# A fourth pair of steps in three feed-forward stages, and two of a pair's weight sums made ahead in DRAM

## The chip, the cores and the metric

One core of a Trainium2 chip runs the whole program. The metric is the device time of one execution in microseconds. Every time of the profile is counted from the start of the span of one profiled execution.

## The reference

Two blocks of a transformer in float32 over 256 positions of width 1024: a gated delta rule, two memory attentions, latent attention, a hybrid mixer, and five feed-forward parts. The change touches the feed-forward parts alone, and where their weights come from:

```python
def swiglu(x, w_gu, w_down):
    gate, up = jnp.split(x @ w_gu, 2, axis=-1)
    return (jax.nn.silu(gate) * up) @ w_down

x = x + 0.5 * swiglu(rms_norm(x, ffn1_norm[l]), ffn1_w_gu[l], ffn1_w_down[l])   # D_MODEL 1024, D_FF 2816
```

## The kernel before

The program is a list of phases (`PHASES`, line 71): ffn0, ain (the delta rule's projections; the recurrence itself runs between them), mem (keys and values of the memories), out0, ffn1, ffn2, bin, uq, out1, ffn3, in2, out2, ffn4. Each phase reads weight tiles of 128 x 2048 float32, 1 MB each. The order of all work is written out by hand, for each engine its own list, and semaphores join the lists.

**A weight tile's way.** SP loads it into one of three raw buffers (`w_raw`, a ring, line 542) when the tile three places before it in the ring has been split (`w_split`). ScalarE rounds it to its high part (`w_hi`, line 584), VectorE takes the rest as its low part (`w_lo`, line 1492). Both parts have three buffers too, so the high part of unit n waits until TensorE has left unit n - 3 (`tile_used`). TensorE does each product as three matmuls: high by high, high by low, low by high (lines 2451 to 2453), with 512 columns in the feed-forward stages.

**A feed-forward stage** has 11 steps of 256 hidden columns. A plain step is two gate-and-up units `g0`, `g1` (for the two halves of the inner dimension, 24 matmuls each) and a down unit `d` (24). Between them four transposes turn the hidden block (lines 2542 and 2602). ffn0, ffn1, ffn3 and ffn4 are `PAIRED`: steps 3 and 4, 6 and 7, 9 and 10 are done as pairs. For a pair, rows (two blocks of 128 positions), inner dimension (two halves) and columns (two steps) form a 2 x 2 by 2 x 2 block product, done with seven products of 12 matmuls in place of eight (Winograd's form): m1, m2, m4 on plain inputs, m6, m7, p3, p5 on sums of inputs (`s_hi_part`, `s_lo_part`), and m4, m6, m7, p5 also on sums of weights. The sums of results (`c11`, `c22`, `c12`) are made by VectorE from snapshots of PSUM that ScalarE takes (`snap`).

**The sums of weights** come in three ways. T1 and T3 are differences of two stored tiles, made in SBUF by GpSimd's queue: a plain load and then a DMA that adds (`pair_sums`, lines 3628 to 3640). T2 = T1 + block and T4 = T2 + block are made by VectorE (`t2`, line 1584, `t4`, line 1590). SP loads the three single blocks into their own buffers (`pair_load`, line 511), so of a pair's weights only the down tiles go through the ring.

**Queues.** SP's loads are one queue, first in, first out. GpSimd's DMAs are another; both share the same 16 DMA engines. ScalarE's and VectorE's lists are in order too: what stands behind a waiting `w_hi` waits with it. In the tail of a stage, ScalarE's order is the last down tile's high part, the next phase's first tile (`w_hi(ends[name])`), then `hidden_hi(10)`. In ain and mem, ScalarE's `w_hi(n0 + 14)` to `w_hi(n0 + 18)` (the four memory tiles and the first of out0) stand between the copies `level_p1` of the delta rule's chain (line 961).

Of the kernel before, what the change touches and what calls it, by code (L numbers as in the profile page):

```python
# [12 lines left out]
P = 128  # L13
SEQ = 256
TB = SEQ // P
# [57 lines left out]
PAIRED = ("ffn0", "ffn1", "ffn3", "ffn4")  # L73
# [25 lines left out]

def stored_at(kind, s):  # L100

    if kind == "d":
        return 3 * STEPS - 1 if s == STEPS - 1 else 3 * s + 4
    return (0 if s == 0 else 3 * s - 1) + int(kind[1])
# [87 lines left out]
def program(nc, d, out):  # L192
# [6 lines left out]
    for name, n in PHASES:  # L199
        tile0[name], stored0[name] = n_tiles, n_stored  # L200
        if name.startswith("ffn"):
            for kind, s in paired_order() if name in PAIRED else plain_order():
                unit_of[name, kind, s] = n_tiles
                if kind in ("g0", "g1", "d"):
                    ring.append((n_tiles, n_stored + stored_at(kind, s)))
# [17 lines left out]
    def last_use(name, half):  # L223

        b = before[name]
        if b.startswith("ffn"):
            return unit_of[b, "p3", STEPS - 2] + 1 if b in PAIRED else unit_of[b, f"g{half}", STEPS - 1] + 1
# [6 lines left out]
    bias_rows = nc.dram_tensor("bias_rows", [P * (ROW + 1)], f32, kind="Internal")  # L234

    with ExitStack() as ctx:
# [81 lines left out]
        PB = [area(S_AT + 2 * TILE + k * TILE, TILE) for k in range(4)]  # L318
        SQ = area(AR_N - 2 * D, TB, D)
# [132 lines left out]

        def pair_no(name, s):
            return len(PAIR_STEPS) * PAIRED.index(name) + PAIR_STEPS.index(s)

        def gates_to(f, s, tb):
            return TB * STEPS * f + GATE_ORDER.index((s, tb)) + 1

        def hiddens_to(f, s, tb):
            return TB * STEPS * f + HIDDEN_ORDER.index((s, tb)) + 1  # L460
# [5 lines left out]
        def pair_source(name, kind, s):  # L466

            if kind == "p5":
# [32 lines left out]
        def _(sp):  # L501
# [11 lines left out]
            def first_loads(kind, name):  # L513

                if kind == "g1":
                    if name != "ffn0":
                        sp.wait_ge(S["x_ready"], 4 * (X_OF[name] - 1) + 1)
                    if name == "ffn3":
                        sp.wait_ge(S["bias_dma"], 16)
                    pair_load(name, PAIR_STEPS[0], 0)  # L520
                    pair_load(name, PAIR_STEPS[0], 2)
                else:
                    sp.wait_ge(S["norm_sd"], norm_no[name] + 1)
                    pair_load(name, PAIR_STEPS[0], 3)

# [11 lines left out]
            for r in range(1, len(ring)):  # L537
                n, t = ring[r]
                if r >= RING:
                    sp.wait_ge(S["w_split"], ring[r - RING][0] + 1)  # L540
                w = width(n)
                sp.dma_start(RAW[:, r % RING, 0:w], d["tiles"][t, :, 0:w]).then_inc(w_loaded[r % RING], 16)
                for name in PAIRED:
# [19 lines left out]
        def _(act):  # L563
# [22 lines left out]
            def pair_ready(name, kind, s):  # L586

                if kind in ("p5", "m7"):
# [91 lines left out]
            def paired_ffn(f, name, first, side):  # L680
# [143 lines left out]
                hidden_hi(10)  # L824
                w_hi(ends[name] + 1)
# [332 lines left out]
            paired_ffn(1, "ffn1", lambda: norm("ffn1"), lambda part: None)  # L1158
# [178 lines left out]
            paired_ffn(3, "ffn3", lambda: norm("ffn3"), lambda part: None)  # L1337
# [130 lines left out]
            paired_ffn(4, "ffn4", lambda: norm("ffn4"), lambda part: None)  # L1468
# [8 lines left out]
        def _(dve):  # L1477
# [81 lines left out]
            def paired_ffn(f, name, start, first, side):  # L1559
# [154 lines left out]
                hidden_lo(10)  # L1714

# [2049 lines left out]
```

## Time and profile before

| | |
|---|---|
| median of 3 runs | 1301.13 us (1301.01 to 1303.16) |
| the profiled execution | 1300.3 us |
| its span | 1298.3 us |
| TensorE busy | 1281.1 us, 99% |
| VectorE busy | 934.5 us, 72% |
| ScalarE busy | 801.0 us, 62% |
| DMA, mean over the span | 205 GB/s, 265.83 MB |
| granted TensorE clock | full, in all slices |

The busy line says which engine's work fills the span; the chain says what the end was waiting for. Since records of matmuls overlap, the distance between two starts is what a matmul costs, and a group's mean is longer. The stages lie at 0 to 192 us (ffn0), 193 to 379 (ain, mem, out0), 379 to 559 (ffn1), 559 to 740 (ffn2), 823 to 1003 (ffn3), 1003 to 1119 (in2, out2) and 1119 to the end (ffn4).

### The profile page before, as it was taken

The page shows a single profiled execution, that of the slowest core. Times are in us where ns is not written, and L with a number is a line of the kernel's source. Part 1 is how long each engine was busy: PE and PEld are TensorE (multiplying, and loading weights), DVE is VectorE, ACT ScalarE, POOL GpSimd, SP SyncE. Part 2 cuts the span into 40 slices and gives each one's busy share as a digit, 9 for nine tenths or more (in the row PEclk, how much of TensorE's full clock was granted, in tenths as well). Part 3 has the DMA queues.
Part 4 walks back from the last instruction along what each step waited for, and adds up shares of the span by engine and source line. Part 5 has one row for each costly group of instructions (what it writes and reads, how often), then busy time and mean ns, then how long its engine had stood idle before and what let it go on. Part 6 is the DMA issues. An engine that isn't in the chain of part 4 may idle for free.

```text
span 1298.3 us, 17145 instructions
## 1 busy us (share of the span) xinstructions
PE 1281.1 (99%) x6976; PEld 1071.9 (83%) x6976; DVE 934.5 (72%) x1091; ACT 801.0 (62%) x1046; POOL 39.8 (3%) x61
## 2 busy tenths in 40 slices
PE   7999999999999999999999999999999999999998
PEld 6888888888988888888787888888888898788887
DVE  5887777777567877866353557678878798688785
ACT  7576658766556665684443466576556757755653
POOL 0000000000000000000000000001000000000000
PEclk9999999999999999999999999999999999999999
DMA  9987635432159778455444532498893534689761
GB/s 354 294 322 227 231 125 195 163 111 87 48 209 339 233 262 290 171 214 202 147 167 146 194 127 73 169 356 260 256 319 103 206 132 151 265 232 328 231 219 33
DMA packets 40206, 265.83 MB, mean 205 GB/s; under 512 B 4476, under 2 KB 6780, under 8 KB 9152
## 3 DMA queue, kind: packets, MB, share of 16 engines
q1 hardware_dynamic: 31056, 205.71, 42.4%
q0 software_dynamic: 7920, 56.37, 16.3%
q10 hardware_dynamic: 1152, 2.66, 0.6%
q8 instruction: 55, 0.90, 0.3%
q14 instruction: 23, 0.19, 0.0%
HBM read 263.67 MB, written 2.11 MB: 205 GB/s over the span
## 4 chain that ended last, share of the span: by engine, by line
PE 95%; ACT 2%; DVE 2%; issue 1%; DMA 0%; SPq 0%; ACTq 0%; DVEq 0%
PE ps L2451 25%; PE ps L2452 25%; PE ps L2453 25%; PE ps L2366 8%; PE ps L2602 1%; PE ps L2377 1%; PE ps L2492 1%; PE ps L2484 1%; PE ps L2497 1%; PE ps L485 1%; PE ps L2507 1%; PE ps L487 1%; PE ps L486 1%; ACT w_hi_part L584 1%; PE ps L2424 1%
## 5 line engine op out<-in xcount | busy, mean ns | idle before, releaser
L1492 DVE TENSOR_TENSOR w_lo_part<-w_raw,w_hi_part 128x2048 fp32r<-128x2048 f32 (+2 forms) x160 | 361.3, 2262 | 135.3 <-ACT w_hi_part L584 135.3
L584 ACT ACTIVATE w_hi_part<-w_raw 128x2048 fp32r<-128x2048 f32 (+2 forms) x159 | 301.4, 1896 | 156.2 <-PE ps L2453 135.1
L2451 PE MATMUL ps<-w_hi_part,x_hi 128*128 128x512 f32 (+1 forms) x800 | 312.3, 390 | 0.8 <-DVE w_lo_part L1492 0.5
L2453 PE MATMUL ps<-w_hi_part,x_lo 128*128 128x512 f32 (+1 forms) x800 | 305.5, 382 | 0.0
L2452 PE MATMUL ps<-w_lo_part,x_hi 128*128 128x512 f32 (+1 forms) x800 | 304.8, 381 | 0.0
L584 ACT ACTIVATE w_hi_part<-arena 128x2048 fp32r<-128x2048 f32 x72 | 138.1, 1918 | 97.4 <-PE ps L2453 93.1
L1492 DVE TENSOR_TENSOR w_lo_part<-arena,w_hi_part 128x2048 fp32r<-128x2048 f32 x72 | 164.6, 2288 | 39.4 <-ACT w_hi_part L584 39.4
L2451 PE MATMUL ps<-w_hi_part,h_hi_part 128*128 128x512 f32 x464 | 186.7, 402 | 0.1
L2453 PE MATMUL ps<-w_hi_part,h_lo_part 128*128 128x512 f32 x464 | 181.4, 391 | 0.0
L2452 PE MATMUL ps<-w_lo_part,h_hi_part 128*128 128x512 f32 x464 | 181.0, 390 | 0.0
L2453 PEld LDWEIGHTS ps<-w_hi_part,x_lo 128*128 128x128 f32 x800 | 150.4, 188 | 29.8
L2451 PEld LDWEIGHTS ps<-w_hi_part,x_hi 128*128 128x128 f32 x800 | 150.5, 188 | 29.5 <-ACT arena L714 1.5
L2452 PEld LDWEIGHTS ps<-w_lo_part,x_hi 128*128 128x128 f32 x800 | 150.7, 188 | 26.7
L2451 PEld LDWEIGHTS ps<-w_hi_part,h_hi_part 128*128 128x128 f32 x464 | 87.2, 188 | 19.3 <-issue 1.9
L2453 PEld LDWEIGHTS ps<-w_hi_part,h_lo_part 128*128 128x128 f32 x464 | 87.1, 188 | 19.0
L2452 PEld LDWEIGHTS ps<-w_lo_part,h_hi_part 128*128 128x128 f32 x464 | 87.2, 188 | 17.7 <-issue 0.5
L2452 PE MATMUL ps<-w_lo_part,s_hi_part 128*128 128x512 f32 x192 | 76.5, 399 | 0.0
L2451 PE MATMUL ps<-w_hi_part,s_hi_part 128*128 128x512 f32 x192 | 75.8, 395 | 0.0
L2453 PE MATMUL ps<-w_hi_part,s_lo_part 128*128 128x512 f32 x192 | 75.3, 392 | 0.0
L2366 PE MATMUL ps<-arena 64*64 64x64 f32 (+7 forms) x636 | 67.6, 278 | 1.6 <-DVE arena L1829 0.8
L2366 PEld LDWEIGHTS ps<-arena 128*128 128x128 f32 (+3 forms) x636 | 54.9, 164 | 9.6 <-issue 3.9
L2451 PEld LDWEIGHTS ps<-w_hi_part,s_hi_part 128*128 128x128 f32 x192 | 36.1, 188 | 9.0
(443 smaller groups left out, 1555.9 us busy)
## 6 DMA issues: line engine op xcount, KB each, us to landing
w_raw<-in_tiles SPq DMA_DIRECT2D x155, 1024.0 KB, 4.9
arena<-in_tiles SPq DMA_DIRECT2D x36, 1024.0 KB, 6.4
arena<-in_tiles POOLq DMA_DIRECT2D x24, 1024.0 KB, 9.6
t<-in_tiles POOLq DMA_DIRECT2D x18, 1024.0 KB, 10.3
mem_kv<-in_tiles POOLq DMA_DIRECT2D x6, 1024.0 KB, 10.4
w_raw<-in_tiles SPq DMA_DIRECT2D x3, 512.0 KB, 5.9
arena<-in_w_ukv POOLq DMA_DIRECT2D x1, 1536.0 KB, 14.3
arena<-in_w_dkv POOLq DMA_DIRECT2D x1, 1280.0 KB, 8.7
```

The source lines that it names most:

```text
L485: nc.tensor.matmul(o, w_hi, a_hi, start=start, stop=False, skip_group_check=True)
L486: nc.tensor.matmul(o, w_hi, a_lo, start=False, stop=False, skip_group_check=True)
L487: return nc.tensor.matmul(o, w_lo, a_hi, start=False, stop=stop, skip_group_check=True)
L584: nc.scalar.activation(WH[:, n % RING, 0:w], source(n), ACT.Copy).then_inc(S["w_hi"], 1)
L1492: nc.vector.tensor_tensor(WL[:, n % RING, 0:w], source(n), WH[:, n % RING, 0:w], ALU.subtract).then_inc(S["w_split"], 1)
L2366: return nc.tensor.matmul(o, w, a, start=start, stop=stop, skip_group_check=True)
L2377: last = nc.tensor.transpose(bank(2 * tb + half)[:, k * P:(k + 1) * P], X[:, tb, kb * P:(kb + 1) * P], con("ident"))
L2424: nc.tensor.matmul(outs[f], part[:, n % RING, at:at + P], XH[:, 4 * g + k, :], start=g == 0 and k == 0 and part is WH, stop=False, skip_gr ...
L2451: nc.tensor.matmul(o, a_hi, w_hi, start=start, stop=False, skip_group_check=True)
L2452: nc.tensor.matmul(o, a_hi, w_lo, start=False, stop=False, skip_group_check=True)
L2453: return nc.tensor.matmul(o, a_lo, w_hi, start=False, stop=stop, skip_group_check=True)
L2484: nc.tensor.matmul(bank(gu_bank(0, tb)), XH[:, 4 * g + k, tb * P:(tb + 1) * P], WH[:, n % RING, k * 512:(k + 1) * 512], start=g == 0 and k ...
```

## The change

ffn1, ffn3 and ffn4 are taken out of `PAIRED` and become `QUADS`: steps 3 and 4, 5 and 6, 7 and 8, 9 and 10 are done as four pairs, one behind the other, with plain steps only for 0, 1 and 2. ffn0 keeps three pairs. In a quad, a pair's products stand in another order (p5, m2, m1, p3, m6, m7, m4, with the down steps of the pair before between them), m2, m1 and p3 read single stored tiles that now go through the ring, and the down step of 9 is the last of the stage.

T1 and T3 of the quads are made in DRAM, in a tensor of their own (`made_sums`, 24 blocks of 1 MB). SP copies the 24 first blocks there: 8 for ffn1 in ffn0's tail, 16 for ffn3 and ffn4 behind the four memory tiles. GpSimd's queue then adds the other blocks in DRAM, 8 for each stage, paced by the splits of ain, ffn2 and in2. In a quad, SP loads the finished sums (`t_load`). T2 is made by VectorE from T1 and the raw tile of p3, in place, and T4 by a DMA of GpSimd's queue that adds a stored tile to it.

```diff
-PAIRED = ("ffn0", "ffn1", "ffn3", "ffn4")
+PAIRED = ("ffn0",)
+QUADS = ("ffn1", "ffn3", "ffn4")
+QUAD_STEPS = (3, 5, 7, 9)
...
+def quad_order():
+    order = [("g0", 0), ("g1", 0), ("g0", 1), ("g1", 1), ("d", 0), ("g0", 2), ("g1", 2)]
+    for s in QUAD_STEPS:
+        order += [("p5", s), ("m2", s), ("m1", s), ("p3", s), ("m6", s), ("d", s - 2), ("m7", s), ("d", s - 1), ("m4", s)]
+    return order + [("d", 10), ("d", 9)]
...
+def ring_kinds(name):
+    return ("g0", "g1", "d", "m1", "m2", "p3") if name in QUADS else ("g0", "g1", "d")
...
+    made = nc.dram_tensor("made_sums", [len(QUADS) * len(QUAD_STEPS), 2, P, TILE], f32, kind="Internal")
...
 SP
+            def copies_after(n):
+                if n == unit_of["ffn0", "d", 8]:
+                    return range(0, 2)
+                if n == unit_of["ffn0", "d", 9]:
+                    return range(2, 5)
+                if n == unit_of["ffn0", "d", 10]:
+                    return range(5, 8)
+                if tile0["mem"] <= n < ends["mem"]:
+                    return range(8 + 4 * (n - tile0["mem"]), 12 + 4 * (n - tile0["mem"]))
+                return ()
+            def copy_block(i):
...
+                sp.dma_start(made[q, k, :, :], d["tiles"][t, :, :], max_dma_last_dim=4 * TILE).then_inc(q_loaded[3], 16)
+            def t_load(name, s, k):
+                dst, (sem, _) = ((TA[QUAD_STEPS.index(s) % 2], t1_loaded(name, s)), (TC, t3_loaded(name, s)))[k]
+                sp.dma_start(dst, made[quad_no(name, s), k, :, :]).then_inc(sem, 16)
...
+                for c in copies_after(n):
+                    if c == 0:
+                        sp.wait_ge(S["w_split"], unit_of["ffn0", "m2", PAIR_STEPS[-1]] + 1)
+                    copy_block(c)
+                for name in QUADS:
+                    if n == unit_of[name, "g1", 1]:
+                        sp.wait_ge(*made_all(name))
+                        sp.wait_ge(S["x_ready"], 4 * (X_OF[name] - 1) + 1)
+                        t_load(name, QUAD_STEPS[0], 0)
...
+                    for s in QUAD_STEPS[1:]:
+                        if n == unit_of[name, "p3", s]:
+                            sp.wait_ge(S["w_split"], unit_of[name, "m7", s - 2] + 1)
+                            t_load(name, s, 1)
...
 VectorE
+                def t2(s):
+                    r = ring_no[at("p3", s)]
+                    dve.wait_ge(S["w_split"], at("p5", s) + 1)
+                    dve.wait_ge(w_loaded[r % RING], 16 * (r // RING + 1))
+                    a = pair_source(name, "m6", s)
+                    nc.vector.tensor_tensor(a, a, RAW[:, r % RING, :], ALU.add).then_inc(S["sums"], 1)
...
 TensorE
+                def quad_of_steps(s):
+                    if s == QUAD_STEPS[0]:
+                        pe.wait_ge(S["sums"], sum_no[name, "s_lo", 0])
+                    s_product("p5", s, 7, True, False)
+                    turn_pair(s - 1 if s == QUAD_STEPS[0] else s - 2)
+                    x_product("m2", s, 5, 0, 1, True, True)
+                    if s > QUAD_STEPS[0]:
+                        turn_pair(s - 1)
+                    x_product("m1", s, 4, 0, 0, True, False)
+                    pe.wait_ge(S["snap"], snaps_to(name, s, 1))
+                    s_product("p3", s, 7, False, True)
+                    pe.wait_ge(S["sums"], sum_no[name, "c11", s])
+                    s_product("m6", s, 4, False, False)
+                    down_half(s - 2, 0)
+                    down_half(s - 2, 1)
+                    pe.wait_ge(S["sums"], sum_no[name, "c12", s])
+                    s_product("m7", s, 4, False, False)
+                    down_half(s - 1, 0)
+                    down_half(s - 1, 1)
+                    if s == QUAD_STEPS[-1]:
+                        turn_pair(10)
+                    pe.wait_ge(S["sums"], sum_no[name, "c22", s])
+                    x_product("m4", s, 4, 1, 1, False, True)
...
 GpSimd
+            def make_sums(name, copied, paced):
+                pool.wait_ge(S["q_loaded3"], 16 * (n_pairs + 2 * len(QUAD_STEPS) * copied))
+                for i, n in enumerate(paced):
+                    s, k = QUAD_STEPS[i // 2], i % 2
+                    pool.wait_ge(S["w_split"], n + 1)
+                    pool.dma_start(made[quad_no(name, s), k, :, :], stored(name, ("g0", "g1")[k], s + 1), accum_op=ALU.add,
+                                   max_dma_last_dim=4 * TILE).then_inc(S["base_loaded"], 16)
+            def t4_sums(name):
+                for s in QUAD_STEPS:
+                    split(name, "m6", s)
+                    pool.dma_start(TA[QUAD_STEPS.index(s) % 2], stored(name, "g1", s), accum_op=ALU.add).then_inc(t4_added(name, s)[0], 16)
...
-            for s in PAIR_STEPS:
-                pair_sums("ffn1", s)
+            make_sums("ffn1", 1, range(tile0["ain"] + 1, tile0["ain"] + 9))
+            t4_sums("ffn1")
...
+            make_sums("ffn3", 3, range(tile0["ffn2"] + 2, tile0["ffn2"] + 26, 3))
...
-            pair_sums("ffn3", PAIR_STEPS[0])
-            pool.wait_ge(S["tile_used"], tile0["ffn3"] + 8)
+            t4_sums("ffn3")
             pool.dma_start(bass.AP(bias_rows, 0, [[ROW + 1, P], [1, ROW]]),
...
+            make_sums("ffn4", 3, range(tile0["in2"] + 1, tile0["in2"] + 9))
+            t4_sums("ffn4")
```

SP's queue, from the last single loads of ffn0 on, before. The block of 24 loads is the rest of ain, mem, out0 and the first units of ffn1; `arena` is the pairs' buffers.

```order
L542 DMA w_raw<-in_tiles 128x2048
L511 DMA arena<-in_tiles 128x2048 x2
L542 DMA w_raw<-in_tiles 128x2048 x4
L542 DMA w_raw<-in_tiles 128x1072 x2
L542 DMA w_raw<-in_tiles 128x2048 x24
```

The same place now. The two loads of 1072 columns are ain's first tiles.

```order
L629 DMA w_raw<-in_tiles 128x2048 x2
L603 DMA made_sums<-in_tiles 128x2048 x2
L629 DMA w_raw<-in_tiles 128x2048
L603 DMA made_sums<-in_tiles 128x2048 x3
L629 DMA w_raw<-in_tiles 128x2048
L603 DMA made_sums<-in_tiles 128x2048 x3
L629 DMA w_raw<-in_tiles 128x1072 x2
L629 DMA w_raw<-in_tiles 128x2048 x13
```

Eight copies now stand between ffn0's last down tiles and ain's first tile. SP's queue in the part behind, whose 13 loads end with the first memory tile (before, all of it is in the row of 24):

```order
L603 DMA made_sums<-in_tiles 128x2048 x4
L629 DMA w_raw<-in_tiles 128x2048
L603 DMA made_sums<-in_tiles 128x2048 x4
L629 DMA w_raw<-in_tiles 128x2048
L603 DMA made_sums<-in_tiles 128x2048 x4
L629 DMA w_raw<-in_tiles 128x2048
L603 DMA made_sums<-in_tiles 128x2048 x4
L629 DMA w_raw<-in_tiles 128x2048 x8
L608 DMA arena<-made_sums 128x2048
```

Four copies stand behind each memory tile, and out0's first tile is the first of the row of eight. VectorE in ffn1's second pair before; L1590 is the sum t4, L1595, L1600 and L1604 are the corrections, L1618 the low part of a hidden block, L1609 a hidden product:

```order
L1492 TENSOR_TENSOR w_lo_part<-w_raw,w_hi_part 128x2048
L1590 TENSOR_TENSOR arena<-arena 128x2048
L1492 TENSOR_TENSOR w_lo_part<-arena,w_hi_part 128x2048
L1595 TENSOR_TENSOR arena<-arena,ps 128x512
L1492 TENSOR_TENSOR w_lo_part<-t,w_hi_part 128x2048
L1618 TENSOR_TENSOR h_lo_part<-ps,h_hi_part 128x512
L1492 TENSOR_TENSOR w_lo_part<-w_raw,w_hi_part 128x2048
L1492 TENSOR_TENSOR w_lo_part<-arena,w_hi_part 128x2048 x2
L1600 TENSOR_TENSOR arena<-ps,arena 128x512
```

VectorE around the second to third pair of ffn1 now, from the correction c22 to m6's low part (L2000 is t2, L2020 a hidden product, L2015 c22, L2029 a hidden block's low part):

```order
L2015 TENSOR_TENSOR arena<-arena,ps 128x512
L1753 TENSOR_TENSOR w_lo_part<-arena,w_hi_part 128x2048 x2
L2000 TENSOR_TENSOR arena<-arena,w_raw 128x2048
L1753 TENSOR_TENSOR w_lo_part<-w_raw,w_hi_part 128x2048
L2020 SCALAR_TENSOR_TENSOR arena<-ps,norm_rsv,arena 128x256
L2020 SCALAR_TENSOR_TENSOR arena<-arena,norm_rsv 128x256
L1753 TENSOR_TENSOR w_lo_part<-w_raw,w_hi_part 128x2048
L2029 TENSOR_TENSOR h_lo_part<-ps,h_hi_part 128x512
L1753 TENSOR_TENSOR w_lo_part<-w_raw,w_hi_part 128x2048
L1753 TENSOR_TENSOR w_lo_part<-arena,w_hi_part 128x2048
```

One sum per pair (t2) is left to VectorE in place of two; it stands between the low parts of p5 and m2, and the two hidden products that the next transposes need stand behind m2's.

## Rows read from the trace of the kernel before

**Rows 1.** The page: busy time per engine, and the chain's shares by engine.

```profile
PE 1281.1 (99%) x6976; PEld 1071.9 (83%) x6976; DVE 934.5 (72%) x1091; ACT 801.0 (62%) x1046; POOL 39.8 (3%) x61
...
PE 95%; ACT 2%; DVE 2%; issue 1%; DMA 0%; SPq 0%; ACTq 0%; DVEq 0%
```

**Rows 2.** Busy time by window: window, length, engines, clock, DMA share, GB/s.

```profile
378.90:558.70 179.80, 179.80 (x820) 147.64 (x817) 142.70 (x122) 111.83 (x115) 9.61 (x14) 1.00 0.78 267
...
555.00:740.00 185.00, 185.00 (x831) 150.56 (x830) 94.83 (x104) 92.21 (x122) 1.07 (x2) 1.00 0.50 175
194.00:355.00 161.00, 156.40 (x1538) 139.35 (x1536) 115.03 (x222) 109.75 (x182) 0.00 (x0) 1.00 0.33 119
```

**Rows 3.** TensorE's timeline in ffn1: start, length, engine, line, shape, count.

```profile
384.94 1.98 PE L2484 MATMUL ps<-w_hi_part,x_hi 128*128 128x512 f32 x8
386.75 1.98 PE L2492 MATMUL ps<-w_lo_part,x_hi 128*128 128x512 f32 x8
```

**Rows 4.** Groups by shape, VectorE, 380 to 540 us: busy us, mean ns.

```profile
L1492 DVE TENSOR_TENSOR w_lo_part<-arena,w_hi_part 128x2048 fp32r<-128x2048 f32 x18 | 41.2, 2288 | 9.7 <-ACT w_hi_part L584 9.7
...
L1584 DVE TENSOR_TENSOR arena<-t,arena 128x2048 f32<-128x2048 f32 x3 | 6.9, 2284 | 0.1
...
L1618 DVE TENSOR_TENSOR h_lo_part<-ps,h_hi_part 128x512 fp32r<-128x512 f32 x9 | 6.2, 685 | 3.8 <-ACT h_hi_part L727 3.8
```

**Rows 5.** VectorE's timeline in ffn1.

```profile
416.68 2.28 DVE L1492 TENSOR_TENSOR w_lo_part<-arena,w_hi_part 128x2048 fp32r<-128x2048 f32 x1
418.88 0.48 DVE L1609 SCALAR_TENSOR_TENSOR arena<-ps,norm_rsv,arena 128x256 f32<-128x256 f32 x1
```

**Rows 6.** Groups by shape, ScalarE, 380 to 540 us.

```profile
L584 ACT ACTIVATE w_hi_part<-arena 128x2048 fp32r<-128x2048 f32 x18 | 34.5, 1918 | 25.9 <-PE ps L2453 25.4 <-DMA arena<-in_tiles 0.5
...
L714 ACT ACTIVATE arena<-ps 128x512 f32<-128x512 f32 x9 | 5.3, 586 | 1.8 <-PE ps L2453 1.8
```

**Rows 7.** Line 3640, the DMAs that add into SBUF, 12 of them.

```profile
DMA to landing us min/median/max: 7.8/8.9/11.4
```

**Rows 8.** The page, DMA issues: count, KB each, median us to landing.

```profile
w_raw<-in_tiles SPq DMA_DIRECT2D x155, 1024.0 KB, 4.9
```

**Rows 9.** DMA, 442 to 444 us: a load into SBUF alone.

```profile
DMA packets 94, 0.77 MB, mean 385 GB/s; under 512 B 0, under 2 KB 0, under 8 KB 0
```

**Rows 10.** DMA, 884.8 to 889.8 us: bias_rows, DRAM to DRAM, alone; 40 slices.

```profile
GB/s 328 197 524 328 393 328 262 524 328 393 197 328 328 262 328 131 393 393 197 0 328 131 262 197 66 197 131 66 66 66 66 131 0 0 66 0 66 0 0 0
DMA packets 143, 1.00 MB, mean 200 GB/s; under 512 B 21, under 2 KB 21, under 8 KB 21
...
q0 software_dynamic: 143, 1.00, 56.8%
```

**Rows 11.** DMA, 880.2 to 884.2 us: an add into SBUF, nearly alone.

```profile
DMA packets 111, 0.90 MB, mean 225 GB/s; under 512 B 1, under 2 KB 1, under 8 KB 1
```

**Rows 12.** VectorE's timeline: low parts of m2 of step 9 and ain's second tile.

```profile
145.71 2.28 DVE L1492 TENSOR_TENSOR w_lo_part<-arena,w_hi_part 128x2048 fp32r<-128x2048 f32 x1
...
194.26 1.26 DVE L1492 TENSOR_TENSOR w_lo_part<-w_raw,w_hi_part 128x1072 fp32r<-128x1072 f32 x1
```

**Rows 13.** SP's loads: ain's first tile, the first and second memory tile.

```profile
173.38 0.33 SPq L542 DMA_DIRECT2D w_raw<-in_tiles  x1
...
254.69 0.33 SPq L542 DMA_DIRECT2D w_raw<-in_tiles  x1
...
261.97 0.33 SPq L542 DMA_DIRECT2D w_raw<-in_tiles  x1
```

**Rows 14.** TensorE's timeline: ffn0's last two down steps start here.

```profile
180.47 0.47 PE L2451 MATMUL ps<-w_hi_part,h_hi_part 128*128 128x512 f32 x1
```

**Rows 15.** ScalarE's timeline: out0's first tile, and what stands behind it.

```profile
311.67 1.90 ACT L584 ACTIVATE w_hi_part<-w_raw 128x2048 fp32r<-128x2048 f32 x1
315.06 0.87 ACT L961 ACTIVATE arena<-ps 128x384 f32<-128x384 f32 x2 [1.49 <-PE ps L2366]
```

More of the change, by code:

```diff
@@ L1156, in sines @@
                     nc.scalar.activation(COS, ANG_C, ACT.Sin).then_inc(S["rope_tab"], 1)
-            paired_ffn(1, "ffn1", lambda: norm("ffn1"), lambda part: None)
+            quad_ffn(1, "ffn1", lambda: norm("ffn1"))
             def kv_turned(u):
@@ L1335, in _ @@
             w_hi(n0 + 9)
-            paired_ffn(3, "ffn3", lambda: norm("ffn3"), lambda part: None)
+            quad_ffn(3, "ffn3", lambda: norm("ffn3"))
             n0 = tile0["in2"]
@@ L1467, in _ @@
             w_hi(n0 + 14)
-            paired_ffn(4, "ffn4", lambda: norm("ffn4"), lambda part: None)
+            quad_ffn(4, "ffn4", lambda: norm("ffn4"))
             for u in range(4):
@@ L2030, in angles @@
                 nc.vector.tensor_scalar(ANG_C, ANG_C, PI_IN, -PI_IN, ALU.min, ALU.max).then_inc(S["rope_ang"], 1)
-            paired_ffn(1, "ffn1", lambda: after_pairs("out0", "ffn1"), lambda: inverse("ffn1"), lambda part: None)
+            quad_ffn(1, "ffn1", lambda: after_pairs("out0", "ffn1"), lambda: inverse("ffn1"))
             def kv_early(s):
@@ L2680, in paired_steps, with quad_gate_up @@
                     down_step(STEPS - 2)
+                def quad_gate_up(s, g):
+                    n = at(f"g{g}", s)
+                    tile_ready(n)
+                    for tb in range(TB):
+                        if g == 0 and s == 2:
+                            pe.wait_ge(S["h_raw"], hiddens_to(f, 1, tb))
+                        for k in range(4):
+                            last = wide(bank(gu_bank(s, tb)), 4 * g + k, tb, n, k * 512, g == 0 and k == 0, g == 1 and k == 3)
+                        if tb == 0 and g == 1:
+                            last.then_inc(S["gu_ps"], 1)
+                    last.then_inc(S["tile_used"], 1)
@@ new lines, in down_half @@
+                def down_half(s, half):
+                    n = at("d", s)
+                    if half == 0:
+                        down_ready(s, n)
+                    for tb in range(TB):
+                        last = down(s, n, half, tb)
+                    if half:
+                        last.then_inc(S["tile_used"], 1)
+                def quad_of_steps(s):
[21 more added lines that the diff above has]
+                    x_product("m4", s, 4, 1, 1, False, True)
@@ L2686, in ffn @@
                     opening(1)
-                for s in range(1, 1 if name in PAIRED else STEPS):
+                for s in range(1, STEPS if name == "ffn2" else 1):
                     gate_up(s, 0)
@@ L3668, in _ @@
                 pool.dma_start(BIAS[:, :, DF_Q[tb]], src).then_inc(S["bias_ready"], 16)
-            for s in PAIR_STEPS:
-                pair_sums("ffn4", s)
+            pool.wait_ge(*made_all("ffn3"))
+            make_sums("ffn4", 3, range(tile0["in2"] + 1, tile0["in2"] + 9))
+            t4_sums("ffn4")
 def layout(a):
```

380 lines of the change are left out of this document (359 added, 21 removed).

## The prediction, made before the changed kernel ran

> **What bounds the kernel now.** I read the page's busy line and chain first: TensorE is busy in 99% of the span and carries 95% of the chain [rows 1]. So time goes only if TensorE's own work goes, or comes if something makes it wait. Next the windows of one paired stage, ffn1: 179.8 us with TensorE busy all through, VectorE 142.70, ScalarE 111.83, the DMA engines at a share of 0.78 [rows 2]. That share is high, but no wait of TensorE stands beside it. Then TensorE's timeline for the true cost of a matmul: eight of 512 columns run from 384.94 to the next at 386.75, so 0.2266 us apiece [rows 3]; the 390 ns of one record overlap the next and must not be used. Then the groups by shape of VectorE and ScalarE in ffn1 [rows 4 to 6], whose work per weight block decides whether TensorE can be fed; and last the landings and rates of the DMAs [rows 7 to 11] and the places where SP's queue meets a due time [rows 12 to 15], since the change leans on both.
>
> **The feed-forward stages.** A pair of steps does 7 block products where two plain steps do 8. A product is 4 blocks of rows times 3 parts, 12 matmuls. ffn1, ffn3 and ffn4 get a fourth pair each, so 3 x 12 = 36 matmuls of 512 columns go (5099 rows on TensorE before, 5063 after): 36 x 0.2266 = 8.16 us, all on the path. Transposes stay at 11 groups a stage. That is the only term that gains.
>
> Does the rest keep up? One pair of the new stage is 7 products of 12 and 2 down steps of 24 matmuls, 132 x 0.2266 = 29.9, and two groups of transposes at about 0.45: 30.8 us. VectorE, by start to start: the instruction behind a low part of 2.28 us starts 2.20 after it, 0.08 overlap [rows 5]; 9 low parts and one sum of the same length make 22.0; three corrections and two low parts of the hidden block at 0.60 (685 ns less 0.08 [rows 4]) 3.0; four hidden products at 0.40 (0.48 less 0.08) 1.6. Together 26.6 of 30.8 us, 86%. ScalarE, less the same overlap: 9 high parts at 1.84, 3 snapshots and 2 high parts of the hidden block at 0.50 [rows 6], 4 gates at about 0.40, 20.7 us, 67%. Both fit on the mean. What is late next is local: five short products stand in a row (p5, m2, m1, p3, m6), and of the three weight buffers a product's copy may start only when the third one ahead has left, so high and low part have 2 x 2.72 = 5.44 us for 1.92 + 2.28 = 4.2. 1.2 us are left, and VectorE puts the sum t2 and two hidden products into just that stretch. Counted from the start T of a pair's last product m4: the down step before it has left, so the next m2 gets its high part from T + 0.3 to 2.2 and its low part to 4.5; TensorE wants it at 2.72 (m4) + 2.72 (p5) + 0.45 = 5.9, 1.4 us later. The two hidden products come behind that low part and end at about 5.3; the transposes that need the first of them are due at 5.44, 0.1 us later. The bounds are 0 and 0.5 us a pair; I take 0.06, so 12 pairs give 0.7 (0 to 6), since in ffn1 before comparable runs show no wait at all [rows 2]. The third buffer's sum t4 is now a DMA that adds into SBUF, issued after m6's low part; ScalarE asks for it 9.8 us later and TensorE 4 us after that. Such adds land in 7.8 to 11.4 us [rows 7]: hidden, nothing taken.
>
> **The copies in the first stage's tail.** SP's queue is first in, first out, so a weight load behind copies waits for them. The price of a 1 MB copy from DRAM to DRAM, r, is not in the trace as such. A load into SBUF alone runs at 385 GB/s, 2.7 us a MB [rows 9]. The one DRAM to DRAM transfer of 1 MB (bias_rows) alone took about 5.0 us from first to last packet, but at 56.8% of the engines, so 2.84 us of all sixteen; its rate falls only where engines run out of work one by one, a tail that a following copy would fill [rows 10]. Bounds: 2.7 and 5.0. I take 2.84, the same row's engine time.
>
> The first copies wait for the split of m2 of step 9, done at 145.71 + 2.28 = 148.0 [rows 12]. From there the queue holds 8 copies, two weight loads (5.4) and the first tile of ain (half a load, 1.4), which lands 2.2 after its last byte (a load's median of 4.9 [rows 8] less 2.7): 157.0 + 8r. Before, it was issued at 173.38 [rows 13]. It is wanted when? The last down step would start at 180.47 + 24 x 0.2266 = 185.9 [rows 14], and before it ScalarE and VectorE must do that tile's high part (1.1), its low part (1.28) and the hidden block's low part (0.7), since the order puts the tile first: 182.7. With r = 2.84 it lands at 179.7, 3.0 us early: no cost. It costs from r = 3.2 on, 8 us per us; at 5.0 it lands at 197.0, 14.3 late.
>
> **The copies in the memory part.** Four behind each of the four memory tiles. From the load at 254.69 [rows 13] the queue holds 16 copies and 5 loads until the first tile of out0 is in: 254.69 + 13.5 + 16r + 2.2 = 270.4 + 16r. The next load comes at 261.97 [rows 13], before four copies can be through, and so do the others. ScalarE takes that tile at 311.67 and needs 1.9 us; behind it in its queue stands the copy of the delta rule's chain at 315.06, for which TensorE waits [rows 15]. So it costs from 272.3 + 16r > 315.06, r = 2.67. At 2.84: 2.7 us; at 5.0: 37 us; at 2.7: 0.4. Before it, 8 sums for ffn1 are added in DRAM, issued behind splits of ain. An add into SBUF alone runs at 225 GB/s, 4.7 us a MB [rows 11]. Eight are 37 us; with ten weight loads of 27 it makes 64 us between the first such split, 194.26 + 1.26 = 195.5 [rows 12], and 254.7 [rows 13], 5 us more than there is, so some 5 us spill into the copies if an add in DRAM costs what it costs in SBUF. No row shows that. Cheaper (0 spill) I can't exclude, nor twice as dear: 37 us more, which would add to rival 2. The copies themselves are the likelier to be cheaper, down to 2.7. So of 2.7 and the 5 us of spill I take 3 in all (0 to 8 with r up to 2.84). The loads of ain land later beside the adds; of that stage's 161 us the DMA engines were busy a third [rows 2], nothing taken (0 to 2).
>
> The remaining moves: adds for ffn3 lie in ffn2 (DMA share 0.50 there [rows 2]) and for ffn4 in in2, behind no wait of TensorE; SP waits in each stage for all of them long after the last is issued. bias_rows moves behind ffn3's adds, its readers stay where they were. In the stages 1 MB less moves per pair. All 0 (0 to 2).
>
> Sum: -8.2 + 0.7 + 3.0 = -4.5. The profiled execution took 1300.3 us with a span of 1298.3; it becomes 1295.8. The median of the runs is 1301.13, 0.8 above the profiled one: 1296.6.
>
> **A page against the row.** The row says 2.84 us of engine time for a MB from DRAM to DRAM [rows 10]. The Trainium skill, page "DMA: Bandwidth & Descriptors", section "Latency and other measured facts", has copies between HBM tensors at 207 to 214 GB/s in each direction at their full rate; by that a copy would be 4.9 us, an estimate from the page, and the sum would come out at the second rival below. The trace's copy alone runs at a mean of 200 GB/s over its 5 us, which agrees, but over 300 in its first two, which does not.
>
> **Rivals.** (1) Copies in between, r of 3.2 to 3.8. For: the row reads the same 8 KB again and again, real copies don't. At 3.6 the tail costs 157.0 + 28.8 - 182.7 = 3.1, the memory part 272.3 + 57.6 - 315.06 = 14.8: +9.7, 1311; at 3.2, 0 + 8.4 + 0.7 - 8.2 = +0.9, 1302. (2) Slower, one mechanism: copies go at the end-to-end pace of the one transfer [rows 10], r = 5.0. 14.3 + 37 - 8.2 = +43, 1344 at worst, 1325 if half of the waits find other work. It decides from r = 3.15, where the gain is gone. Against: the dense start of the copy's window. (3) The saved products come back as waits in the new pairs, so that the change does not do what it says: VectorE at 86%, margins of 0.1 us; at 0.5 us for each of 12 pairs 6 us, with the memory part +0.8, 1302. Against: 0.78 DMA share and no wait in ffn1 before. (4) No cost anywhere: 1293.0.
>
> **Chances.** Forecast, with what lies around it (1292.5 to 1298.5, r up to 2.9): 0.52, rival 4's 1293 within it. Rival 1: 0.20. Rival 2: 0.17. Rival 3: 0.11. The measurement tells about 0.2%, 2.6 us, from no change, so under 1298.5 is faster, over 1303.7 slower. Faster: 0.50 of the first case and 0.02 of rival 1, 0.52. Same: 0.02 + 0.07 of rival 1 + 0.08 of rival 3, 0.17. Slower: 0.31. The range is 1292 to 1315: 1 or 2 in 100 lie below, rival 2 above.
>
> **What would show it.** Right: ffn1, ffn3 and ffn4 each 2.7 us shorter than 179.8, no wait of TensorE over 0.3 us in the pairs; the copies landing about 2.8 us apart; ScalarE's copy of out0's first tile some 3 us behind its place, and the span from ain to ffn1's start longer by as much. Wrong: ScalarE waiting for w_raw's DMA at ain's first tile or at the memory tiles by 5 us and more (rival 2), or VectorE's low parts named before TensorE's idle in the pairs (rival 3).

## The result: 1.2% slower, and the profile after

The changed kernel takes 1317.38 us (median of 4 runs, 1316.74 to 1321.6) against 1301.87 us of the kernel before on the same chip: ratio 1.0121, 95% interval 1.0101 to 1.0141, so 15.8 us slower (0.0121 x 1302). Forecast were 1296.6 us and a range that ended at 1315.

The page of the changed kernel, busy line, chain, DMA totals and landings (times of rows 1 and 8 before):

```profile
span 1314.9 us, 17160 instructions
PE 1281.5 (97%) x6940; PEld 1069.6 (81%) x6940; DVE 948.9 (72%) x1103; ACT 820.4 (62%) x1064; POOL 44.6 (3%) x61
...
DMA packets 46686, 313.02 MB, mean 238 GB/s; under 512 B 5196, under 2 KB 7500, under 8 KB 9872
...
PE 81%; DMA 9%; DVE 4%; ACT 4%; issue 1%; SPq 1%; ACTq 0%; DVEq 0%
...
w_raw<-in_tiles SPq DMA_DIRECT2D x179, 1024.0 KB, 6.3
made_sums<-in_tiles SPq DMA_DIRECT2D x24, 1024.0 KB, 20.3
made_sums<-in_tiles POOLq DMA_DIRECT2D x24, 1024.0 KB, 16.1
```

TensorE has 36 matmuls fewer and is busy no shorter, though its share fell from 99 to 97%: that needs a second cause, the clock, below. The chain gained 9% of DMA, where it had none [rows 1], and a weight load lands in 6.3 us in place of 4.9 [rows 8]. To see where the time went, I match the same instruction in both timelines. TensorE before, at four places (the end of ain's first two tiles, the memory attention, the key heads in ffn2, in2):

```profile
198.22 1.15 PE L2773 MATMUL ps<-w_hi_part,x_lo 128*128 128x268 f32 x8
337.06 1.00 PE L2366 MATMUL ps<-mem_kv,t 128*128 128x64 f32 x8
615.08 4.47 PE L2366 MATMUL ps<-arena,t 128*128 128x320 f32 x16
1044.92 7.07 PE L2366 MATMUL ps<-arena 128*128 128x256 f32 x32
```

The same four in the changed kernel:

```profile
204.02 1.15 PE L3256 MATMUL ps<-w_hi_part,x_lo 128*128 128x268 f32 x8
357.84 1.00 PE L2779 MATMUL ps<-mem_kv,t 128*128 128x64 f32 x8
634.21 4.47 PE L2779 MATMUL ps<-arena,t 128*128 128x320 f32 x16
1062.01 7.07 PE L2779 MATMUL ps<-arena 128*128 128x256 f32 x32
```

The differences are +5.8, +20.8, +19.1 and +17.1 us. So the first stage lost 5.8, ain to memory 15.0, and the quads of ffn1 and ffn3 gave back 1.7 and 2.0. Of the 5.8, 2.0 were lost by 58 us, ahead of all copies (the transposes at 56.28 before start at 58.25); there the other profiles come out 0.2 us earlier to 1.0 later with nothing changed either, so 3.8 are left for the tail. The last transposes of out2 start at 1115.55 before and at 1134.61 now, +19.1, and the span is 16.6 longer: in2 and out2 took 2.0, and ffn4 gave back 2.5. Within the 15.0, a second match at the memory keys (301.71 before, 315.77 after) puts 8.3 us into ain and 6.7 into the memory part.

**Ain.** TensorE waits 7.5 us in one place, where 1.2 us stood before. Its timeline there, first before, then around it in the changed kernel (the bracket is idle time, and who ended it):

```profile
215.45 1.09 PE L2798 MATMUL ps<-consts,arena 128*128 128x128 f32 x8 [1.16 <-ACT arena L915]
```

```profile
219.72 0.39 PE L2866 MATMUL ps<-w_hi_part,x_lo 128*128 128x512 f32 x1
227.65 1.97 PE L3281 MATMUL ps<-consts,arena 128*128 128x128 f32 x8 [7.54 <-ACT arena L1176]
```

It names a copy of ScalarE, but in ScalarE's order that copy stands behind a weight tile's high part, and this one waits for its load:

```profile
225.11 1.91 ACT L694 ACTIVATE w_hi_part<-w_raw 128x2048 fp32r<-128x2048 f32 x1 [4.80 <-DMA w_raw<-in_tiles]
226.93 0.67 ACT L1176 ACTIVATE arena<-ps,norm_rsv 128x512 f32<-128x512 f32 x1
```

The DMA view of 210 to 225 us says why. Its columns are packets, MB and the share of 16 engines that the packets took; q0 is GpSimd's queue with the adds, q1 SP's with the loads:

```profile
q0 software_dynamic: 287, 2.09, 66.9%
q1 hardware_dynamic: 288, 2.10, 34.7%
...
w_raw<-in_tiles SPq DMA_DIRECT2D x3, 1024.0 KB, 18.3
```

The last row is a load: three of 1 MB, and their median time from issue to landing in us. Both queues moved the same number of packets, but an add's packet takes twice the time. A block is 1.049 MB, so an add costs 0.669 x 15 / 2.09 x 1.049 = 5.0 us of all engines, near the 4.7 of [rows 11], and a load 0.347 x 15 / 2.10 x 1.049 = 2.6. With as many packets from one queue as from the other, a load beside adds comes at one block in 15 / 2.10 x 1.049 = 7.5 us in place of 2.7 [rows 9], and lands in 18.3. Before, four loads between 196 and 215 us landed in 4.8. The Trainium skill, page "DMA: Bandwidth & Descriptors", section "Queues, rings and completion order", says that a DMA engine goes round the queue rows that have work and drains a whole packet from each before it moves on. The counts 287 and 288 agree; what the Trainium skill calls a packet can hold several of the profile's packets of 8 KB, and these counts can't tell how long a turn is. The forecast didn't use it.

**The tail and the memory part.** ScalarE, at ain's first tile and at out0's:

```profile
186.99 1.10 ACT L694 ACTIVATE w_hi_part<-w_raw 128x1072 fp32r<-128x1072 f32 x1 [7.43 <-DMA w_raw<-in_tiles]
...
335.10 1.91 ACT L694 ACTIVATE w_hi_part<-w_raw 128x2048 fp32r<-128x2048 f32 x1 [9.27 <-DMA w_raw<-in_tiles]
```

The first copy of the tail was issued at 149.99, 2.0 us after the forecast's 148.0, so by the forecast's sum the tile lands at 159.0 + 8r = 186.99, and r comes to 3.5 us. Part of this is not the copies' own: between 150 and 187 us ScalarE's queue moves 0.84 MB of constants, 6.2% of the engines' time or 2.3 us, which the forecast left out. Without them r is 3.2, an estimate, right at its limit. In the memory part the first load stands at 268.95, 14.3 later than before; 284.65 + 16r = 335.10 gives r = 3.15. Both lie above the limits that the forecast had worked out, 3.2 and 2.67.

**in2.** The same pattern, beside the last of ffn4's adds (issued at 1087.96): ScalarE waits 5.5 us for a load, and TensorE 1.8.

```profile
1091.68 1.92 ACT L694 ACTIVATE w_hi_part<-w_raw 128x2048 fp32r<-128x2048 f32 x1 [5.51 <-DMA w_raw<-in_tiles]
```

**The clock.** The column before the last two is the granted clock. Before it was full in all slices; now it is half, 1.2 in place of 2.4 GHz, for some microseconds of work behind the pauses of 2.0 us (to 190.15) and 7.5 us, and once more from 346 us on:

```profile
190.00:194.00 4.00, 3.85 (x10) 3.11 (x11) 0.69 (x1) 0.27 (x1) 0.00 (x0) 0.58 0.73 285
222.00:227.00 5.00, 0.00 (x0) 0.00 (x0) 0.00 (x0) 1.89 (x2) 0.67 (x1) 0.78 1.03 280
227.00:231.00 4.00, 3.35 (x12) 3.07 (x13) 2.29 (x1) 1.94 (x6) 0.81 (x1) 0.50 1.03 281
346.00:351.00 5.00, 5.00 (x40) 4.93 (x37) 1.87 (x4) 1.77 (x6) 0.00 (x0) 0.67 0.04 16
```

Not every pause did this: behind those of 1.7 us (to 337.82) and 1.8 us (in in2) the clock stayed full, and between 338 and 346 us stands none above 1.0. Where it did, a pause costs more than its own length: the group of eight at 227.65 takes 1.97 us where it took 1.09. Two rough estimates agree on what it cost in all. A mean granted clock of 0.994 over 1314.9 us is 7.9 us lost; and the busy time rose by 0.4 us where 36 matmuls less should have taken 8.2 off it.

### The profile page after: what moved, and what is told of

Read it like the earlier page. It is cut to its first block, busy times and chain, and to the rows that moved or that the text cites. A ratio compares the mean times of both kernels' runs of the same rounds, so it can differ in the third digit from the quotient of the medians.

```text
span 1314.9 us, 17160 instructions
## 1 busy us (share of the span) xinstructions
PE 1281.5 (97%) x6940; PEld 1069.6 (81%) x6940; DVE 948.9 (72%) x1103; ACT 820.4 (62%) x1064; POOL 44.6 (3%) x61
## 2 busy tenths in 40 slices
DMA packets 46686, 313.02 MB, mean 238 GB/s; under 512 B 5196, under 2 KB 7500, under 8 KB 9872
## 4 chain that ended last, share of the span: by engine, by line
PE 81%; DMA 9%; DVE 4%; ACT 4%; issue 1%; SPq 1%; ACTq 0%; DVEq 0%
PE ps L2864 22%; PE ps L2865 22%; PE ps L2866 22%; DMA w_raw<-in_tiles 8%; PE ps L2779 5%; DVE w_lo_part L1753 2%; ACT w_hi_part L694 1%; PE ps L3015 1%; PE ps L2790 1%; PE ps L2897 1%; PE ps L2905 1%; PE ps L2910 1%; DMA arena<-in_tiles 1%; SPq L603 1%; PE ps L2837 1%
## 5 line engine op out<-in xcount | busy, mean ns | idle before, releaser
L1753 DVE TENSOR_TENSOR w_lo_part<-w_raw,w_hi_part 128x2048 fp32r<-128x2048 f32 (+2 forms) x184 | 416.2, 2267 | 137.5 <-ACT w_hi_part L694 137.5
L694 ACT ACTIVATE w_hi_part<-w_raw 128x2048 fp32r<-128x2048 f32 (+1 forms) x183 | 346.3, 1896 | 171.7 <-PE ps L2866 123.4
L2864 PE MATMUL ps<-w_hi_part,x_hi 128*128 128x512 f32 (+1 forms) x740 | 290.2, 392 | 1.6 <-DVE w_lo_part L1753 1.2
L2866 PE MATMUL ps<-w_hi_part,x_lo 128*128 128x512 f32 (+1 forms) x740 | 282.7, 382 | 0.0
L2865 PE MATMUL ps<-w_lo_part,x_hi 128*128 128x512 f32 (+1 forms) x740 | 281.9, 381 | 0.0
L694 ACT ACTIVATE w_hi_part<-arena 128x2048 fp32r<-128x2048 f32 x66 | 126.0, 1916 | 66.7 <-PE ps L2866 37.1
L1753 DVE TENSOR_TENSOR w_lo_part<-arena,w_hi_part 128x2048 fp32r<-128x2048 f32 x66 | 150.2, 2288 | 22.5 <-ACT w_hi_part L694 22.1
L2865 PE MATMUL ps<-w_lo_part,s_hi_part 128*128 128x512 f32 x240 | 95.7, 399 | 0.0
L2864 PE MATMUL ps<-w_hi_part,s_hi_part 128*128 128x512 f32 x240 | 94.7, 395 | 0.0
L2866 PE MATMUL ps<-w_hi_part,s_lo_part 128*128 128x512 f32 x240 | 94.1, 392 | 0.0
L2864 PEld LDWEIGHTS ps<-w_hi_part,s_hi_part 128*128 128x128 f32 x240 | 45.1, 188 | 11.2
```

What stands on the lines that cost most here:

```text
L694: nc.scalar.activation(WH[:, n % RING, 0:w], source(n), ACT.Copy).then_inc(S["w_hi"], 1)
L1753: nc.vector.tensor_tensor(WL[:, n % RING, 0:w], source(n), WH[:, n % RING, 0:w], ALU.subtract).then_inc(S["w_split"], 1)
L2864: nc.tensor.matmul(o, a_hi, w_hi, start=start, stop=False, skip_group_check=True)
L2865: nc.tensor.matmul(o, a_hi, w_lo, start=False, stop=False, skip_group_check=True)
L2866: return nc.tensor.matmul(o, a_lo, w_hi, start=False, stop=stop, skip_group_check=True)
```

## The experiments

Each time is a median, and the ratio, with its 95% interval, is to the kernel before on the same chip (1302.84 us for the quads alone, no adds, the sums of ffn1 only and the plain copies; 1302.36 for the copies in another queue and the tail's copies alone; 1302.64 for the rest). The microseconds behind a ratio are (ratio - 1) x 1302. The kernels with adds or copies left out (the quads alone, no adds, the sums of ffn1 only, plain copies, half the copies, the tail's copies alone) do not compute the reference: where a sum is left out, a quad multiplies a single block, with the same bytes loaded into SBUF.

### The quads alone

```diff
-                sp.dma_start(dst, made[quad_no(name, s), k, :, :]).then_inc(sem, 16)
+                sp.dma_start(dst, d["tiles"][stored0[name] + stored_at("g0", s + k), :, :]).then_inc(sem, 16)
```

with all calls of `copy_block` and `make_sums` removed.

> The sums of weights are left out altogether: no copy and no add in DRAM, and each quad loads the first stored block where it would load the finished sum, so the same bytes reach SBUF. Theory A (the three quad stages do gain, and the traffic that makes the sums costs all of the loss and more): with the 5.8, 8.3, 6.7 and 1.9 us by which the first stage, ain, the memory part and in2 came out later in the changed kernel gone, 1317.4 - 22.7 = 1294.7, range 1293 to 1297. Theory B (the quads themselves give nothing, waits inside the pairs eat the 8.2 us): 1300 to 1303.

Measured: 1294.37 us, ratio 0.9936 (0.9914 to 0.9958), -8.3 us. The quads gain, within the interval what the matmuls promised; everything that made the change slower, 24 us, is the transfers that make the sums.

### No adds

`make_sums` removed, SP waits for the copies in place of the adds.

> The copies stay where they are, the 24 adds in DRAM are left out (the quads load the copied blocks, waiting for the copies). Theory A (in ain it is the add that starves the weight loads: each of its 8 KB packets holds a DMA engine for 628 ns, a load's for 309 to 324): ain and in2 give back 8.3 and 1.9 us, tail and memory part keep their cost, 1307, range 1305 to 1309. Rival (a backlog of the copies is what delays ain's loads): ain stays as late as it is, 1315 to 1317.

Measured: 1304.87 us, ratio 1.0020 (1.0003 to 1.0037), 13.2 us below the changed kernel, a little more than the 10.2 expected. TensorE's wait in ain was 1.1 us, as before. The copies, with no adds beside them, still cost 11.

### The sums of ffn1 only

```diff
-                if tile0["mem"] <= n < ends["mem"]:
-                    return range(8 + 4 * (n - tile0["mem"]), 12 + 4 * (n - tile0["mem"]))
...
-            make_sums("ffn3", 3, range(tile0["ffn2"] + 2, tile0["ffn2"] + 26, 3))
...
-            make_sums("ffn4", 3, range(tile0["in2"] + 1, tile0["in2"] + 9))
```

> The sums of ffn3 and ffn4 are left out (their quads load single stored blocks): no copies behind the memory tiles, no adds in ffn2 and in2. The eight copies in the first stage's tail and the eight adds in ain stay. Theory A (16 copies at 3.15 us against a deadline met up to 2.67 us): the memory part gives back 6.7, in2 1.9: 1308.8, range 1307 to 1311. Rival (the memory part is late because ain's adds pushed SP's queue, not because of its own copies): only in2's 1.9 comes back, 1315 to 1316.

Measured: 1306.54 us, ratio 1.0037 (1.0017 to 1.0057). The sums of ffn3 and ffn4 cost 10.9 us, a little more than the 8.6 expected; ain's wait stood nearly unchanged at 7.7.

### Plain copies in place of ain's adds

```diff
-                    pool.dma_start(made[...], stored(name, ("g0", "g1")[k], s + 1), accum_op=ALU.add,
+                    pool.dma_start(made[...], stored(name, ("g0", "g1")[k], s + 1),
+                                   **({} if name == "ffn1" else {"accum_op": ALU.add}),
```

> Only the eight adds for ffn1 become plain copies of the same blocks to the same place, in the same queue, paced the same (so ffn1's weight sums are wrong). Theory A (an add's packet holds the engine twice as long, and each engine takes the queues in turn): packets of this queue fall to about 310 to 400 ns, SP's loads get half of the engines in place of a third, and of ain's 8.3 us about 5 come back: 1312, range 1310 to 1314. Rival (a second queue beside the loads costs the same whatever it does, or the wait is not the DMA's share): 1316 to 1318.

Measured: 1312.74 us, ratio 1.0072 (1.0052 to 1.0092), 6.4 us less. TensorE's wait in ain fell from 7.5 to 3.8 us. The DMA view of 210 to 220 us:

```profile
q1 hardware_dynamic: 282, 2.06, 52.7%
q0 software_dynamic: 257, 1.88, 46.0%
...
w_raw<-in_tiles SPq DMA_DIRECT2D x3, 1024.0 KB, 11.0
```

Now the engines are shared about half and half, SP moves 2.06 MB in 10 us in place of 2.10 in 15, and a load lands in 11.0 us in place of 18.3. So the price has two parts: a second queue takes about every other packet, and an add's packet is twice as long.

### The same adds, later

```diff
-            make_sums("ffn1", 1, range(tile0["ain"] + 1, tile0["ain"] + 9))
+            make_sums("ffn1", 1, [tile0["ain"] + k for k in (7, 8, 9, 10, 11, 12, 12, 13)])
```

> Only the pacing of ffn1's eight adds changes: they wait for the splits of ain's 8th to 14th tile in place of its 2nd to 9th. Theory A (the adds cost because they stand beside ain's first five weight tiles, whose loads have some 9 us each): the wait of 7.7 us in ain goes with the half clock behind it, 8 us less, but the last adds now reach into the memory part, where the copies already are late, and 3 to 6 us come back there: 1313, range 1310 to 1316. Rival (an add costs wherever it stands beside loads of ain): 1316 to 1320.

Measured: 1329.34 us, ratio 1.0207 (1.0185 to 1.0228), 11 us more than the change and far outside both expectations. Ain's wait did go (1.1 us). But the last four adds now run beside SP's copies, and the weight loads stand behind those copies. The DMA view of 280 to 294 us, and the waits of 255 to 372 us (engine, line, for whom, total, times, longest):

```profile
q0 software_dynamic: 229, 1.72, 68.6%
q1 hardware_dynamic: 235, 1.66, 32.1%
...
made_sums<-in_tiles SPq DMA_DIRECT2D x3, 1024.0 KB, 38.2
```

```profile
ACT w_hi_part L694 <- DMA w_raw<-in_tiles: 44.6, 4, 14.0
```

A block in SP's queue takes 14 / 1.66 x 1.049 = 8.8 us there, and four copies ahead of each load multiply that: 44.6 us of waits in four tiles, TensorE stands for 13.0, 5.1 and 5.2 us. The expectation had added the bytes of both queues; the sum that fits is SP's queue alone at a third of the engines.

### Half the copies in the memory part

```diff
-                    return range(8 + 4 * (n - tile0["mem"]), 12 + 4 * (n - tile0["mem"]))
+                    return range(8 + 2 * (n - tile0["mem"]), 10 + 2 * (n - tile0["mem"]))
```

> Behind each memory tile stand two copies in place of four, ffn3's; ffn4 has no copies and no adds (its quads load single stored blocks). Theory A (a due time: 8 copies at 3.15 us end long before out0's first tile is wanted, the limit is 13 to 14 copies): the memory part costs nothing at all, as with no copies there: the same as the run with ffn1's sums only, 1306.5, range 1305 to 1308.5. Rival (the copies' cost is in proportion to their number, by contention): half of the 6.7 us stays, 1310.

Measured: 1308.22 us, ratio 1.0051 (1.0031 to 1.0071), against 1306.54 (1.0037) with none. The interval is too wide to tell the 1306.5 of the first expectation from the rival's 1310. The timeline can, at the memory keys and the memory attention, the same two places as above:

```profile
315.48 0.93 PE L2781 MATMUL ps<-arena 64*64 64x64 f32 x48 [0.86 <-DVE arena L2244]
350.83 1.00 PE L2781 MATMUL ps<-mem_kv,t 128*128 128x64 f32 x8
```

They lie 35.35 us apart, as before the change (301.71 to 337.06) and as with no copies there (314.96 to 350.31, the sums of ffn1 only); with sixteen copies it is 42.07 (40.37 without the adds). ScalarE waits for no weight there. So eight copies cost nothing in the memory part and sixteen cost 5 to 7 us: a due time, not a price per copy.

### The copies in another queue

The 16 copies are issued by GpSimd, paced by the same splits:

```diff
+            for i in range(16):
+                pool.wait_ge(S["w_split"], tile0["ain"] + 11 + i // 4 + 1)
+                ...
+                pool.dma_start(made[quad_no(name, s), k, :, :], stored(name, "g0", s + k),
```

> The 16 copies of the memory part leave SP's queue for GpSimd's, issued when SP issued them, the rest is as in the changed kernel. Theory A (the copies cost because the weight loads stand behind them in one first-in first-out queue; beside a copy in another queue a load gets half of the engines, 5.4 us a MB, and four of them are needed in 40 us): the 6.7 us of the memory part come back, 1310.5, range 1309 to 1312.5. Rival (the bytes cost in any queue): 1316 to 1318.

Measured: 1309.1 us, ratio 1.0063 (1.0036 to 1.0089), 7.6 us less than the change. In the memory part ScalarE's waits for weights are gone from the list, and the two places above lie 35.34 us apart. The bytes are the same, but no weight load stands behind a copy: between 268 and 310 us a load lands in 11.3 us, against 17.6 in the changed kernel.

### The tail's copies alone

Only the eight copies of the tail stay.

> Of all the transfers that make the sums only the eight copies in the first stage's tail stay; no adds, no copies in the memory part (quads load the copied or single blocks). Theory A (in the changed kernel TensorE waits 2.2 us for ain's first tile and then works at half clock for some 3 us): 1294.4 + 2.2 + 1.5 = 1298, range 1296.5 to 1300. Rival (the tail is covered, as was forecast, and what was seen there comes from the saturated start of the stage): 1294 to 1295.5.

Measured: 1300.29 us, ratio 0.9980 (0.9968 to 0.9992), 5.7 us above the quads alone. ScalarE waited 7.8 us for ain's first tile, TensorE 2.4 us, and the clock was half from about 190 to 194 us. So the tail was not covered. The run lies just above the range of the first expectation, and the 5.7 carries some 3 us of uncertainty. The timelines are sharper: between the transposes near 57 us and the end of ain's first two tiles, the eight profiles with the tail's copies take 2.7 to 5.4 us more than the kernel before, the three without them (the quads alone, the sums elsewhere, ffn1 in three pairs) at most 0.1 more or less.

### The sums elsewhere

All 24 copies go to GpSimd's queue (`copy_sums`, paced by splits as `make_sums` is); each step waits until the one before has landed:

```diff
+            copy_sums("ffn1", [tile0["ain"] + k for k in (6, 7, 8, 8, 9, 10, 10, 11)])
+            make_sums("ffn1", [tile0["ain"] + k for k in (11, 12, 12, 13, 14, 15, 15, 16)])
...
+            copy_sums("ffn3", range(tile0["ffn2"] + 1, tile0["ffn2"] + 9))
+            make_sums("ffn3", range(tile0["ffn2"] + 10, tile0["ffn2"] + 26, 2))
+            copy_sums("ffn4", range(tile0["ffn2"] + 25, tile0["ffn2"] + 33))
...
+            make_sums("ffn4", range(tile0["bin"], tile0["bin"] + 8))
```

> The whole change, with every copy and add kept but in other places: all 24 copies go from SP's queue to GpSimd's; ffn1's eight are paced by the splits of ain's 7th to 12th tile and its adds by the last ain and the first memory tiles; ffn3's copies and adds stand in ffn2, ffn4's copies at ffn2's end and its adds in bin, uq and out1. Theory A (not the bytes cost, only where they meet weights that are due within a few us): nearly as fast as the quads without any sums, 1294.4 plus 0 to 3, 1296, range 1294 to 1299. Rival (48 MB more through the same 16 engines cost wherever they stand, in half clock and late loads): 1303 or more.

Measured: 1295.97 us, ratio 0.9952 (0.9933 to 0.9971), -6.3 us: faster than both kernels, and 2.1 us by the ratios from the quads without any sums, which is within the uncertainty. Its page:

```profile
span 1294.4 us, 17163 instructions
...
DMA packets 46686, 313.02 MB, mean 242 GB/s; under 512 B 5196, under 2 KB 7500, under 8 KB 9872
...
PE 91%; ACT 3%; DVE 3%; DMA 2%; issue 1%; SPq 0%; ACTq 0%; DVEq 0%
```

It moves the same 46686 packets and 313.02 MB as the changed kernel, with a span 20.5 us shorter. Seven of ffn1's eight adds run beside the memory tiles' loads (issued between 265 and 293 us), and loads land in 11.9 us there. But each is issued some 20 us before ScalarE takes it, out0's first tile at 292.0 and 314.2, and no copy stands in SP's queue.

### ffn1 in three pairs

As the kernel above, but ffn1 stays as before the change.

> As the kernel with the sums elsewhere, but ffn1 is done as before, with three pairs and its sums in SBUF: no copy and no add in DRAM ahead of ffn2. Theory A: two of three saved groups of products remain, 2 x 2.7 = 5.4 us below the kernel before, which stood at 1302.8 in the last call: 1297.4, range 1295.5 to 1299.5. If it is under the kernel with all three, ffn1's sums cost more than the 2.7 us that its fourth pair gives. Rival (ffn2 and bin to out1 can't take 32 transfers unseen): 1301 or more.

Measured: 1298.82 us, ratio 0.9973 (0.9959 to 0.9986), 2.7 us above the kernel with all three by the ratios, with some 3 us of uncertainty; a fourth pair was forecast to be worth 2.7. So with the sums well placed ffn1's pair looks like a gain too, but this is not shown clear of the noise.

## Why the prediction was wrong

The forecast was -4.5 us; the change cost 15.8. Four kernels, each with one more part of the transfers than the last, split this into -8.3 (quads) + 5.7 (tail) + 7.4 (adds in ain, 1.0037 - 0.9980) + 10.9 (sums of ffn3 and ffn4). That they add up follows from the way they are formed and proves nothing; each carries 3 to 4 us of uncertainty.

1. **The saved matmuls: right, a little short.** Forecast -8.2 + 0.7; measured -8.3 (5.5 to 11.2). In the timelines the three stages give 1.7, 2.0 and 2.5 of 2.7 us, 6.2 in all: the matched places lie 278.02 us apart before and 276.37 after (ffn1), 429.84 and 427.80 (ffn3). Where the rest went is open; no wait of TensorE in a pair exceeded 0.3 us. VectorE kept up, T4's add was hidden. Rival 3 is out.
2. **The loads of ain beside the adds, "nothing taken (0 to 2)": the step that failed most, 7.4 us.** It argued from a mean: DMA busy a third of 161 us [rows 2]. But the loads that matter there are those of the five tiles behind ain's first whole one, due early and close together (with the quads alone their low parts start at 203.4, 206.2, 212.5, 215.3 and 224.6 us), while the adds are paced by the same tiles' splits and so start just when the next load does. And where it did add up the queues, it took 2.7 us for a load: beside an add it is 7.5. The matched places put the loss in ain at 8.3 us; without the adds the wait is gone, and with plain copies in their place it is 3.8 us.
3. **The price of a copy: r = 2.84 taken, 3.15 measured in the memory part, 3.5 in the tail.** The formulas around it held: the limits of 3.2 and 2.67 decided both places. The tail's term was 0 and is 5.7 by the runs, 3.8 in the changed kernel's timeline: r passed its limit, in part because the constants in ScalarE's queue were left out, and the half clock came on top. The memory part's was 3.0, whose 2.7 of copies by its own formula is 16 x (3.15 - 2.67) = 7.7, as measured (7.6 from the queue's change, 6.7 in the timeline). The engine time of one lone transfer [rows 10] was too low for where it was used: among weight loads, 276 to 300 us, q1 moved 8.14 MB in 24 us at a share of 100.3%, 3.1 us a block. Its 5 us of spill of the adds did not come: the last add had landed by 263, before the copies began at 269.
4. **The adds in ffn2 and in2, 0: half right.** Nothing new waited in ffn2; in2 and out2 lost 2.0 us.
5. **The Trainium skill on copies.** By the 207 to 214 GB/s of the Trainium skill, page "DMA: Bandwidth & Descriptors", section "Latency and other measured facts", r would be 4.9, an estimate. Copies alone moved 2.10 MB between 271 and 276 us, 419 GB/s, 2.5 us a block. Those figures, which the Trainium skill gives for rows that lie 512 KiB and more apart, do not hold for these blocks, which lie in one piece; the measurement decides, and rival 2 is out. Rival 1's r was right, and its sum (1302 at 3.2) still 15 us short, for want of step 2 and the clock.
6. **The clock: not in the forecast at all.** It counted a wait as its own length; by the two estimates above, some 8 us were lost to the half clock.

A small slip stands in the recorded sums: the tail's due time is 182.8 by its own terms, not 182.7, which changes nothing.

What stays open: the 10.9 us of ffn3's and ffn4's sums are 7.6 + 2.0 from the places named, and the last 1.3 lie within the uncertainty. How much of each pause's cost is wait and how much is half clock was read from the windows, not tested apart. The kernel with the sums elsewhere moved them to another queue and to other stretches at once; only for the sixteen copies of the memory part was the queue changed alone.

## What to carry to other kernels

A transfer is not priced by its bytes but by what stands behind it in its queue and beside it on the engines: work out for each due time in its neighbourhood the pace of that queue alone, with what was measured here left to it: one packet in two, which beside an add is one third of the time. A mean DMA share over a stage says nothing of its first tiles. The same transfers cost 24 us in one place and about 2 in another, so put them where loads are issued well before they are used (some 20 us here), in a queue where nothing waits behind them.

## What the runs showed of the hardware that was not expected

The half clock also came without any wait. In the kernel with the quads alone and in the kernel before, TensorE does the same narrow matmuls near 250 us, busy all through. First the window of the kernel before and its group of 14, then those of the quads alone:

```profile
248.00:256.00 8.00, 8.00 (x52) 7.23 (x52) 7.86 (x20) 3.28 (x4) 0.00 (x0) 1.00 0.15 50
...
249.82 1.81 PE L2366 MATMUL ps<-arena 128*128 128x128 f32 x14
```

```profile
249.00:257.00 8.00, 8.00 (x36) 7.35 (x36) 7.86 (x21) 2.09 (x3) 0.00 (x0) 0.57 0.11 33
...
250.84 3.33 PE L2774 MATMUL ps<-arena 128*128 128x128 f32 x14
```

The same group took 1.81 us at full clock and 3.33 at half, with groups of one column and of 128 ahead of it in both. From ain's third tile to the memory keys this made the stretch 3.2 us longer (105.06 against 101.85), with no change to the work in it. Four of the twelve profiles show it (no adds 3.10 us, the tail's copies alone 3.22, the sums elsewhere 3.17), the others have 1.81. What sets it off stays open. So check a difference of 3 us between two single profiles against the granted clock before you put it down to an edit.
